# First layer: tile 0 takes all 1024 value columns from gathered rows, instead of 640 gathered and 384 from a dense gate matrix

## What is computed

```python
    def block(args):
        xb, eb, gb = args
        act = jax.nn.gelu(jnp.einsum('thkd,td->thk', peer_u[eb], xb), approximate=False) * gb
        return jnp.einsum('thk,thkd->td', act, peer_v[eb])
```

## Time and profile before

| | us |
|---|---|
| median of 3 runs | 2063.33 |
| lowest, highest | 2059.63, 2063.72 |
| span of the profiled execution | 2058.1 |
| PE busy in it | 1900.5 (92%) |
| DVE busy | 1377.4 (67%) |
| ACT busy | 901.4 (44%) |
| POOL busy | 773.3 (38%) |
| bytes moved | 622.89 MB, mean 303 GB/s |

### The profile page before, as it was taken

The page is one execution under the profiler, slowest core; times in us unless marked ns, Lnnn a source line. Parts: engine busy times, 40 slices in busy tenths (PEclk is TensorE's granted clock), DMA queues, the critical chain, the costliest instruction groups (busy, mean ns, idle before and its releaser), DMA issues. The chain is left out here.

```text
span 2058.1 us, 32947 instructions
## 1 busy us (share of the span) xinstructions
PE 1900.5 (92%) x12722; PEld 1667.2 (81%) x12722; DVE 1377.4 (67%) x2723; ACT 901.4 (44%) x1945; POOL 773.3 (38%) x626
## 2 busy tenths in 40 slices
PE   6999999987888989999999999898898899899998
PEld 6999988887888989776666889898897899677774
DVE  6643431379889948588785244168798888688884
ACT  5545443123335737544442454103233668544442
POOL 0000000058676634344441000037677555444441
PEclk9999999998999999999999999999999999999999
DMA  6433453899999988999997334679999998899996
GB/s 231 162 121 114 161 198 132 347 357 342 384 372 409 384 319 290 330 379 401 397 394 271 133 134 144 245 313 378 408 393 404 356 325 286 296 378 388 391 389 253
DMA packets 154298, 622.89 MB, mean 303 GB/s; under 512 B 19207, under 2 KB 22919, under 8 KB 138782
## 3 DMA queue, kind: packets, MB, share of 16 engines
q1 hardware_dynamic: 96798, 402.65, 51.9%
q0 software_dynamic: 57344, 218.14, 27.8%
HBM read 619.66 MB, written 1.05 MB: 302 GB/s over the span
## 5 line engine op out<-in xcount | busy, mean ns | idle before, releaser
L1013 PE MATMUL bank<-nt_sb,ut_sb 128*128 128x128 f32 x4096 | 505.3, 280 | 47.0 <-DMA ut_sb<-in_ut_dram 42.5
L1013 PEld LDWEIGHTS bank<-nt_sb,ut_sb 128*128 128x128 f32 x4096 | 483.9, 196 | 58.5 <-DMA ut_sb<-in_ut_dram 42.8
L2328 POOL DMA_INDIRECT big_sb<-in_u_dram,idx_sb x256 | 254.1, 993 | 243.6 <-ACT big_sb L1177 115.2
L1177 ACT ACTIVATE big_sb<-bank 128x512 f32<-128x512 f32 (+11 forms) x282 | 131.4, 479 | 330.9 <-PE bank L1013 108.1
L2292 POOL TENSOR_TENSOR sm_sb<-sm_sb,vec_sb 128x1 f32<-128x1 f32 (+2 forms) x24 | 19.4, 812 | 637.6 <-DVE sm_sb L1682 632.0
L2103 DVE CUSTOM_DVE_ANT_0 big_sb<-big_sb,bank_n 128x1024 f32<-128x1024 f32 x170 | 205.4, 1210 | 52.1 <-DMA big_sb<-in_u_dram,idx_sb 47.9
L2351 POOL TENSOR_TENSOR big_sb<-big_sb,nt_sb 128x1024 f32<-128x1024 f32 x86 | 204.3, 2377 | 10.7 <-DMA big_sb<-in_u_dram,idx_sb 7.7
L631 PE MATMUL bank<-n_hi,w_hi 128*128 128x256 f32 x608 | 180.4, 297 | 13.6 <-DVE w_lo L1679 13.4
L1177 ACT ACTIVATE big_sb<-big_sb 128x1024 f32<-128x1024 f32 (+2 forms) x132 | 116.5, 884 | 152.9 <-POOL big_sb L2351 139.5
L1065 PE MATMUL bank_n<-v_hi,g_hi 128*128 128x384 f32 x240 | 177.4, 739 | 0.0
L2328 POOL DMA_INDIRECT cst_sb<-in_vl_dram,idx_sb x102 | 120.9, 1185 | 144.6 <-DVE x_sb L1685 141.5
(11 more groups left out here) (270 smaller groups left out, 4069.0 us busy)
## 6 DMA issues: line engine op xcount, KB each, us to landing
ut_sb<-in_ut_dram SPq DMA_DIRECT2D x256, 512.0 KB
big_sb<-in_wall_dram SPq DMA_DIRECT2D x119, 1024.0 KB, 9.9
nt_sb<-in_v_dram SPq DMA_DIRECT2D x130, 512.0 KB
sw_sb<-in_v_dram SPq DMA_DIRECT2D x84, 512.0 KB
ab_sb<-in_v_dram SPq DMA_DIRECT2D x42, 512.0 KB
big_sb<-in_u_dram,idx_sb POOLq DMA_INDIRECT x256
cst_sb<-in_vl_dram,idx_sb POOLq DMA_INDIRECT x102
spare_sb<-in_vl_dram,idx_sb POOLq DMA_INDIRECT x102
```

The costliest lines, as they stand in the source:

```text
L1013: i = e.matmul(hs(bk, c % 4), UT[:, c % DR, k * 128:(k + 1) * 128], TN[1][:, k, :], start=k == 0, stop=k == 7)
L1177: return e.activation(out, in_, func, bias=bias, scale=scale, **kw)
L2328: return e.indirect_dma_start(out, None, table, bass.IndirectOffsetOnAxis(ap=IDX[:, k:k + 1], axis=0))
```

## The change

Layer 1 is put into a list `FULL`. For a layer in it:

- tile 0 takes whole rows of 1024 value columns. POOL gathers them into the eight `UB` places, DVE adds them to `x_sb` 1024 wide;
- `gates(1, 0)`, `experts(1, 0)` and `sums_out(1, 0)` are gone from all engines, and so is tile 0's part of every value step: 120 slices of `g_hi` and `g_lo` are 128 wide instead of 256, PE loses the 384-wide products, and the tail has 8 steps instead of 16, so 8 part loads go;
- 38 rows are placed ahead of the first value step, the other 90 at 2.85 beats each (value steps have 2.1);
- tile 0's norm `fin` follows its last row; the first scaling of `n2` for tile 0 now waits for the last value step, because it writes where `GM[:, 1]` lies;
- the weights for `keys` no longer wait for a value step.

The core of the diff (`lows` and `norm_2` are DVE's, `value_rows` is POOL's, `weights2` is SP's):

```diff
+FULL = (1,)
+T_VAL = {1: (768, 2.1, 2.85), 2: (1713, 2.4, 3.2)}
+T_ROW = {1: (590, 4.6), 2: (1536, 4.6)}
+EARLY = 38
 def low_beat(l, n):
+    if l in FULL:
+        return T_ROW[l][0] + T_ROW[l][1] * n if n < EARLY else T_VAL[l][0] + T_VAL[l][2] * (n - EARLY)
...
+        steps = lambda l: [(c, (1,)) for c in CORD] if l in FULL else BOTH
+        last = lambda l, t: 127 + TAIL * (t == 1 and l not in FULL)
...
             def weights2():
                 for n in range(4):
                     yield 860 + 32 * n
-                    e.wait_ge(*val_v.at("gl", 1, STEPS.index((79 + 16 * n, (0, 1)))))
+                    if 1 in FULL:
+                        e.wait_ge(*sel_p.at("q", 1, 1, 7))
...
             def lows(l):
                 for n in range(128):
                     yield low_beat(l, n) + 6
-                    dst = X[:, 0, 0:FD]
+                    dst = X[:, 0, :] if l in FULL else X[:, 0, 0:FD]
...
+                        e.wait_ge(*u_in[n % UR].at(l, 128 + n))
...
             def norm_2():
...
                     yield from mean(("n2", t), (b, b + 0.8))
+                    if t == 0 and 1 in FULL:
+                        e.wait_ge(*val_p.at("whole", 1, last(1, 1)))
                     yield from scaled(("n2", t), XS2[t], X[:, t, :], (b + 2, b + 2.4))
...
+            def value_rows(l):
+                for n in range(128):
+                    yield low_beat(l, n)
+                    if n < UR:
+                        e.wait_ge(*(dot_a if pooled(128 + n - UR) else dot_v).at("dot", l, 128 + n - UR))
+                    else:
+                        e.wait_ge(*low_v.at(l, n - UR))
+                    gather(UB[n % UR], a[f"vl{l}"], n).then_inc(*u_in[n % UR].up(l, 128 + n))
...
-        "u1": f("peer_u")[0], "ut1": chunked(f("peer_u")[0]), "vl1": f("peer_v")[0][:, :FD], "v1": f("peer_v")[0].reshape(128, 128, D).transpose(1, 0, 2),
+        "u1": f("peer_u")[0], "ut1": chunked(f("peer_u")[0]), "vl1": f("peer_v")[0], "v1": f("peer_v")[0].reshape(128, 128, D).transpose(1, 0, 2),
```

More of the change, by code:

```diff
@@ L595, in values @@
                 table = a[f"v{l}"]
[L596 to L597 removed]
+                for s, (c, ts) in enumerate(steps(l)):
+                    yield max(dense_beat(l, 125), gate_out(l, gated(l)[0], 30)) + s if s < 6 else T_VAL[l][0] + T_VAL[l][1] * (s - 5)
                     if s < 2 or s == 5:
[L599 removed]
+                        e.wait_ge(*gate_p.at("mm", l, gated(l)[0], 31))
                     elif s < 5:
@@ L1035, in values @@
             def values(l):
-                for s, (c, ts) in enumerate(STEPS):
+                for s, (c, ts) in enumerate(steps(l)):
                     b = s % 2
                     n = len(ts)
+                    whole = s >= 128 - TAIL
                     gh, gl = [x[:, b, 0:n * 128].rearrange("p (a t) -> p a t", a=n) for x in (GH, GL)]
@@ L1563, in values @@
             def values(l):
-                for s, (c, ts) in enumerate(STEPS[:128 - TAIL]):
+                for s, (c, ts) in enumerate(steps(l)[:128 - TAIL]):
                     b, n = s % 2, len(ts)
@@ L1584, in final @@
             def final(l, t):
-                b = T_VAL[l][0] + T_VAL[l][1] * LAST[t] + 4.5
-                yield from squares(("fin", l, t), X[:, t, :], (b, b + 0.4), [[fin_v.at("fin", l, 1, 0) if t else low_v.at(l, 127)], [fin_v.at("fin", l, t, t)]])
+                b = T_VAL[l][0] + T_VAL[l][1] * last(l, t) + 4.5
+                if t == 0 and l in FULL:
+                    b = low_beat(l, 127) + 8
+                yield from squares(("fin", l, t), X[:, t, :], (b, b + 0.4), [[fin_v.at("fin", l, 1, 0) if t else low_v.at(l, 127)],
+                                                                             [fin_v.at("fin", l, 1, 1) if t else low_v.at(l, 127) if l in FULL else fin_v.at("fin", l, 0, 0)]])
             def norm_2():
@@ L1989, in final @@
             def final(l, t):
-                b = T_VAL[l][0] + T_VAL[l][1] * LAST[t] + 5
+                b = T_VAL[l][0] + T_VAL[l][1] * last(l, t) + 5
+                if t == 0 and l in FULL:
+                    b = low_beat(l, 127) + 8.5
                 yield from mean(("fin", l, t), (b, b + 0.8))
@@ L2309, in norms @@
                 yield from rstd(("peer", 1, 1), 290.5 + LATER)
-                yield from rstd(("fin", 1, 0), 1042.5)
+                yield from rstd(("fin", 1, 0), low_beat(1, 127) + 9)
+                yield from rstd(("fin", 1, 1), T_VAL[1][0] + T_VAL[1][1] * last(1, 1) + 6)
                 yield from rstd(("n2", 0), 1046)
-                yield from rstd(("fin", 1, 1), 1077.5)
                 yield from rstd(("n2", 1), 1080)
@@ L2315, in norms @@
                 yield from rstd(("peer", 2, 1), 1279.5)
-                yield from rstd(("fin", 2, 0), T_VAL[2][0] + T_VAL[2][1] * LAST[0] + 6)
-                yield from rstd(("fin", 2, 1), T_VAL[2][0] + T_VAL[2][1] * LAST[1] + 6)
+                yield from rstd(("fin", 2, 0), T_VAL[2][0] + T_VAL[2][1] * last(2, 0) + 6)
+                yield from rstd(("fin", 2, 1), T_VAL[2][0] + T_VAL[2][1] * last(2, 1) + 6)
             def gdn(t):
```

58 lines of the change are left out of this document (34 added, 24 removed).

## The result

| | before | after |
|---|---|---|
| median of 4 runs, us | 2061.5 | 2095.4 |
| lowest, highest | 2058.4, 2063.7 | 2090.7, 2101.7 |
| span of the profiled execution | 2058.1 | 2088.8 |
| PE busy in it | 1900.5 | 1855.8 |
| HBM read, MB | 619.7 | 643.3 |

After takes 1.0164 times as long, 95% interval 1.0142 to 1.0186: slower by 1.6%. PE works 45 us less and 23.6 MB more are read. The medians lie 34 us apart, the two profiled executions 31 us. The median of the kernel before has one run more than the table ahead of the prediction. The profiled execution of after is the fastest of its four, 4.7 us under the median.

A forecast was written before the change was run, and what follows sets the result against it. PE was taken to bound the value steps with 24 GB/s of DMA unused, DMA after the change; 10 us of loads plus 10 us of exposed norm give a 2078 us span, 2083 us as median, range 2069 to 2096.

The forecast's parts named there:

- E: The end of PE's value products in layer 1, forecast at about 1140 us against 1129.8 before.
- PE's 62 us: Layer 1's value steps: 0.52 us of PE products removed per step, 120 times; no gain expected, as DMA becomes slowest.
- Bytes: Layer 1's value loads: wider gathers add 25.2 MB, dropped part loads save 1.6 MB, net 23.6 MB.
- The rate: DMA from 740 us to the last value chunk was taken to move 405 GB/s.
- term one: End of layer 1's value steps: PE ends at about 1140 us instead of 1129.8, 10 us later.
- 159.1 MB / 405: Loads from 740 us to the last value chunk, divided by DMA's rate in GB/s: 393 us, landing at 1133 us.
- The block of 23 rows: Ahead of layer 1's first value step: DVE adds 23 rows in 31 us, PE idle for 25 to 35 us.
- Value steps: In layer 1, DMA needs 2.25 us per step, against 1.9 for DVE and 1.56 for PE.
- Term two: Behind layer 1's last value product: tile 0's norm, hidden before, is exposed, delaying `keys(1)` by 10 us (7 to 12).
- Rivals 1 and 2: Layer 1's value loads: faster DMA, DVE sets pace, 2037 us, chance 3%; DMA slightly better, norms overlap better, 2065, 5%.
- Rival 3: Value steps: PE's waits keep its clock at 1.2 GHz, 2185 us; chance 4% for more than 15 us.
- Rival 4: Value-row gathers: whole rows cost DMA no more than before; 2% better per unit, already in the 405; no chance given.

The follow-up runs named there:

- e4: Changed kernel with three more 384-column PE products in each of the 120 value steps, into a bank nobody reads; 2099.3 us, 1.0186 of the kernel before.
- e2: Changed kernel whose gathers fetch 640 of 1024 value columns, DVE still adding 1024; 2053.4 us, 0.9954 of the kernel before.
- e5: Changed kernel with rows sooner, at 2.9 beats instead of 4.6 and 60 ahead of the first value step; 2092.7 us, 1.0156 of the kernel before.
- e8: Changed kernel whose gathers fetch 832 of 1024 value columns, DVE still adding 1024; 2076.5 us, 1.0069 of the kernel before.
- e3: Changed kernel where DVE adds only 640 of each row's 1024 gathered columns, gathers whole; 2097.0 us, 1.0165 of the kernel before.
- e1: Changed kernel with tile 0's second norm placed elsewhere and ordered ahead of the last value steps; 2085.8 us, 1.0116 of the kernel before.
- e6: Changed kernel with 15 rows instead of 38 ahead of the first value step, the rest spread over the steps; 2095.7 us, 1.0157 of the kernel before.

## Why the prediction was right, and where it was off

The direction and the mechanism held: the loads from 740 us on and the uncovered norm are the loss. The median of 2095 us is inside the range, but only just, 12 us above the 2083 that was predicted. The loss was forecast at 20 us and measured at 31 by the profiled executions, 34 by the medians. The 12 us add up so: 8 at E (1147.9 for 1140), 1 in the norm, 2 behind `keys(1)` (span 2088.8 where the first two give 2087), 1 because the median of after lies 6.6 us above the span and not 5.2.

- **PE's 62 us are worth nothing** because DMA takes over: right. e4 puts them back at a cost of some 4 us that can't be told from none, and e2 takes the bytes away and gains 42. The premise was rough: in the kernel before I took 383 GB/s and 24 free, but in the middle of its value steps it moved 394, so that DMA was nearer to its bound than I said.
- **Bytes**: predicted net 23.6 MB, read 643.25 - 619.66 = 23.6 MB.
- **The rate is the term that was mis-sized.** I took 405 GB/s for everything from 740 us on. The value steps gave 409 and the block 388, but the first 80 us gave 363. (405 - 363) x 80 us = 3.4 MB, 8 us, which is the size of the miss of term one: 18 us instead of 10. Smaller ones cancel: 820 to 840 us gave only 341 GB/s, 3 us more, and the 409 of the value steps gave as much back. The last bytes landed near 1142 us instead of 1135. The reasoning behind it, that DMA fills up wherever bytes are wanted, left out that bytes must also have a free place to land in. In 600 to 680 us DMA was full while row places came free quickly: 33 gathers were issued in those 80 us of the kernel before, against 21 from 740 to 820 us of after. That this is the cause is supported by e5 and not proved. The test that the prediction set itself, 400 GB/s or more in every 20 us from 750 us, failed in this stage and pointed to the place.
- **"159.1 MB / 405"** failed in a second way, shown by e8 and e2 and not visible in the total: not every byte behind 740 us has the same worth. By the sum 25.2 MB were worth 62 us; taking them away gave 42. The count that fits, made afterwards, is that bytes behind the first value step count in full and those ahead of it count for nothing when they are fewer, since DVE then sets the block and the few free places the dense stage. The sum still fitted after within 12 us because in its block of rows DVE's time for a row and DMA's are equal (e3): there nearly all bytes counted.
- **The block of 23 rows**: predicted 31 us with PE idle for 25 to 35, measured 30.4 and 29.1. A row of 1024 columns: predicted 1.3 to 1.4 us, measured 1.279. The first value step can't be finished before 852, I said, and its `g_lo` was at 857.5: the dense products, which I had ended at 820, ended at 827, the slow dense stage again.
- **Value steps**: predicted 2.25 us, DMA's pace, measured 2.31 in the mean. The 409 GB/s and the waits for `in_v` show that it is DMA's.
- **Term two**: predicted 10 us, `keys(0)` 8 us behind E and `keys(1)` 25.7 behind it; measured 9.1 and 26.7, together 10.9. e1 takes it away and gains 9.5 by the medians. The estimate of 2 us for the cold start was near: 15.81 against 13.98 us for 64 products.
- **Rivals 1 and 2** needed 435 and 420 GB/s. The highest 20 us of after moved 412. The DMA page of the Trainium skill ("DMA: Bandwidth & Descriptors", Bandwidth) has 425 for a 16 MB transfer; this traffic, one core's 4 KB rows and 512 KB chunks together, did not reach it. Only a few us without row gathers come near: 422 GB/s in the kernel before, shown at the end.
- **Rival 3**, the low clock, came in part and was free: the granted clock is 0.94 in the value steps, not 1.00. Ahead of the 3.34 us wait shown above and right behind it the windows read:

```profile
1070.00:1075.00 5.00, 4.08 (x10) 1.72 (x10) 3.51 (x7) 1.66 (x4) 1.87 (x2) 1.00 1.02 415
1078.00:1082.00 4.00, 4.00 (x8) 2.01 (x8) 2.67 (x5) 1.61 (x4) 0.83 (x1) 0.58 1.04 383
```

The 0.58 is close to the lower of the two levels, 1.2 GHz. The granted clock swings for some us (0.50 from 1080 to 1082, 0.99 from 1082 to 1084, 0.50 from 1086 to 1088) and is 1.00 from 1090 us on. PE is busy 234 of 272 us in the value steps, so it has room for it.
- **Rival 4**, that whole rows are cheaper for DMA, is true by 1.5% (403, 403 and 409 GB/s with 640, 832 and 1024 columns from 900 to 1090 us), about what was in the 405.

## What to carry to other kernels

Before trading one engine's work for bytes, read the GB/s of the very stage that gets the bytes, and divide: here 4 to 6% of DMA were free, 32 more columns gained 0.3%, 384 more turned the bound around and lost 1.6%. A full rate measured in one stage need not hold in another, so count the places that turn over and ask who empties them. When profiles of the same code differ by several us, compare distances within each one. And when a step loses its work, look for what used to hide under it: a third of this loss was a norm that had lost its cover, and ordering it a little earlier brought nearly all of that third back.

## What the runs showed of the hardware

- The core's DMA gave 409 GB/s at a share of 1.03 in the value steps of after, rows and chunks together, for 272 us on end, and 363 GB/s at a share of 0.97 in its dense stage, where POOL waited for free row places in 43.6 of 80 us. A share near 1 is therefore no proof that no more would go through: with more rows ordered there the same stage gave 384 at 0.99 (e5). And 1.03 is not the same rate everywhere: in the kernel before, with chunks loading and no row gather issued since 1096 us, it went with 422 GB/s:

```profile
1118.00:1122.00 4.00, 4.00 (x10) 1.71 (x9) 1.10 (x3) 0.00 (x0) 0.55 (x1) 1.00 1.03 422
```

- A PE that waits for its data in most steps was granted 0.94 of the clock in after, 0.95 in the steps of e5 and 0.94 in those of e6. In after, once the norm had kept it idle for most of 9 us, 64 products took 15.81 us instead of 13.98.
- From 900 to 1090 us the mixture moved at 409 GB/s with rows of 4096 bytes, at 403 with rows of 3328 and of 2560 bytes.
- Adding one row times a weight took DVE 0.88 us for 640 columns and 1.279 us for 1024.
